# Recurrent heads of a two-block model on one core: full 32-bit gate products replaced by three products of high and low parts

## The reference

```python
def block_diag(x, w, b):          # 10 heads of 128 channels, w is (10, 128, 128)
    y = jnp.einsum('bshi,hij->bshj', x.reshape(bsz, s, h, i), w)
    return y.reshape(bsz, s, h * j) + b

def rglru_direction(xc, wa, ba, wx, bx, lam, reverse):
    r = jax.nn.sigmoid(block_diag(xc, wa, ba))
    i = jax.nn.sigmoid(block_diag(xc, wx, bx))
    log_a = -LRU_C * r * jax.nn.softplus(-lam)
    a = jnp.exp(log_a)
    b_in = jnp.sqrt(-jnp.expm1(2.0 * log_a)) * (i * x32)
    _, h = lax.associative_scan(_lin_combine, (a, b_in), axis=1, reverse=reverse)
```

## Time and profile before

| what | value |
|---|---|
| median of 3 runs | 3472.39 us |
| the profiled execution | 3469.35 us |
| its span, first to last instruction | 3468.0 us |
| TensorE (PE) busy | 3346.8 us, 97% of the span |
| VectorE (DVE) busy | 2045.6 us, 59% |
| ScalarE (ACT) busy | 1390.2 us, 40% |
| GpSimd (POOL) busy | 1317.9 us, 38% |
| mean granted TensorE clock | 0.993 of full speed |

### The profile page before, as it was taken

One profiled execution on the slowest core, in us unless ns is written; L12 is line 12 of the kernel. 1 busy time (PEld: TensorE's weight loads), 2 busy tenths in 40 slices (PEclk: granted clock), 3 DMA queues, 4 the chain that ended last, 5 costly groups with the idle time before them and its releaser, 6 DMA issues.

```text
span 3468.0 us, 48887 instructions
## 1 busy us (share of the span) xinstructions
PE 3346.8 (97%) x19926; PEld 2718.9 (78%) x19926; DVE 2045.6 (59%) x2689; ACT 1390.2 (40%) x2361; POOL 1317.9 (38%) x698
## 2 busy tenths in 40 slices
PE   7999999999989999999999999999999999999999
PEld 6788888897668778878887677777788877777787
DVE  3656737427754743345555538986544588888654
ACT  4443334344433544431113447772233343444212
POOL 3212222110024444454442116663344365656542
PEclk9999999999999999999999999999999999999999
DMA  5101111020036344442222322223465423333522
GB/s 153 43 19 47 42 33 48 26 62 7 1 110 213 107 138 143 142 174 97 97 97 87 103 90 67 82 83 107 163 196 172 135 88 109 106 111 106 188 96 81
DMA packets 343791, 344.40 MB, mean 99 GB/s; under 512 B 14661, under 2 KB 263937, under 8 KB 343568
## 3 DMA queue, kind: packets, MB, share of 16 engines
q1 hardware_dynamic: 328960, 307.00, 27.7%
q10 hardware_dynamic: 11520, 25.17, 1.9%
q0 software_dynamic: 3088, 9.10, 0.7%
HBM read 268.86 MB, written 72.35 MB: 98 GB/s over the span
## 4 chain that ended last, share of the span: by engine, by line


## 5 line engine op out<-in xcount | busy, mean ns | idle before, releaser
L461 POOL TENSOR_TENSOR weight_lo<-stage,weight_hi 128x1024 fp32r<-128x1024 f32 (+4 forms) x269 | 626.5, 2336 | 991.9 <-ACT weight_hi L439 963.1
L2459 DVE TENSOR_TENSOR x<-x,psum 128x512 f32<-128x512 f32 x416 | 283.9, 687 | 281.7 <-PE psum L403 271.2
L439 ACT ACTIVATE weight_hi<-stage 128x1024 fp32r<-128x1024 f32 (+4 forms) x329 | 299.7, 925 | 334.2 <-PE psum L403 289.8
L401 PE MATMUL psum<-hT_hi,weight_hi 128*128 128x512 f32 x1024 | 411.0, 401 | 1.5 <-DVE hT_lo L654 1.5
L402 PE MATMUL psum<-hT_lo,weight_hi 128*128 128x512 f32 x1024 | 400.2, 391 | 0.0
L403 PE MATMUL psum<-hT_hi,weight_lo 128*128 128x512 f32 x1024 | 400.1, 391 | 0.0
L401 PE MATMUL psum<-weight_hi,act_hi 128*128 128x512 f32 x864 | 337.3, 390 | 5.3 <-POOL act_lo L2407 4.2
L402 PE MATMUL psum<-weight_lo,act_hi 128*128 128x512 f32 x864 | 336.8, 390 | 0.0
L403 PE MATMUL psum<-weight_hi,act_lo 128*128 128x512 f32 x864 | 336.7, 390 | 0.0
L461 POOL TENSOR_TENSOR weight_lo<-sum,weight_hi 128x512 fp32r<-128x512 f32 (+1 forms) x114 | 238.2, 2099 | 233.8 <-ACT weight_hi L439 233.8
L401 PE MATMUL psum<-T_hi,weight_hi 128*128 128x512 f32 x608 | 238.6, 392 | 18.5 <-POOL weight_lo L461 14.5
(11 more groups left out here) (421 smaller groups left out, 7098.0 us busy)
## 6 DMA issues: line engine op xcount, KB each, us to landing
stage<-in_w_up SPq DMA_DIRECT2D x66, 512.0 KB, 4.3
stage<-in_w_in SPq DMA_DIRECT2D x64, 512.0 KB, 4.0
act_raw<-scratch_act SPq DMA_DIRECT2D x54, 512.0 KB, 5.2
stage<-in_w_ffn_up SPq DMA_DIRECT2D x48, 512.0 KB, 4.6
scratch_gates<-gate ACTq DMA_DIRECT2D x64, 256.0 KB, 2.0
gs<-scratch_gates SPq DMA_DIRECT2D x64, 256.0 KB, 3.1
stage<-in_w_out SPq DMA_DIRECT2D x32, 512.0 KB, 4.5
scratch_act<-out SPq DMA_DIRECT2D x64, 256.0 KB, 4.7
```

What stands on the lines that cost most here:

```text
L401: q.matmul(out, stat[0], mov[0], start=first, stop=False, skip_group_check=onto)
L439: a.q.activation(hi[:, part], src, ACT.Copy).then_inc(*S.w_hi.up(w))
L461: g.q.tensor_tensor(lo[:, part], src, hi[:, part].bitcast(F32), ALU.subtract).then_inc(*S.w_lo_pool.up(w))
L2459: v.q.tensor_tensor(dst, dst, K.bank(key), ALU.add).then_inc(*S.x.up(("f", f, g, t, n)))
```

## The change

The gate products go through `three`, so each of the 8 products of a head is three matmuls instead of one plain float32 call. For this a new step `head_split` stands at the head of each round of the loop, ahead of the next head's front. In it ScalarE makes the high parts of `xc` (128x1024) and of the four block weights (128x512), and GpSimd the two low parts by subtraction. The low parts of the block weights are written over the block weights themselves, which stay two buffers; the high parts and the low part of `xc` have one buffer each. The wait of the gate products for the load and for the convolution becomes a wait for ScalarE's and GpSimd's block weight parts.

```diff
 def pe_head_gate(K, j, i, h):
     b = K.open(key)
-    pe.wait_ge(S.wbd_load[j % 2], j)
-    pe.wait_ge(S.dve_op, ("xc", j))
-    pe.q.matmul(b, K.wbd[j % 2][:, i, :], K.xc[j % 2][:, h * HALF:(h + 1) * HALF], start=True, stop=True).then_inc(*S.mm.up(key))
+    pe.wait_ge(S.act_op, ("wbd_hi", j))
+    pe.wait_ge(S.pool_op, ("wbd_lo", j))
+    at = slice(h * HALF, (h + 1) * HALF)
+    three(pe.q, b, (K.wbd_hi[:, i, :], K.wbd_lo[j % 2][:, i, :]), (K.xc_hi[:, at], K.xc_lo[:, at]), True, True).then_inc(*S.mm.up(key))
+
+def act_head_split(K, j):
+    a, S = K.a, K.S
+    a.wait_ge(S.dve_op, ("xc", j))
+    if j:
+        a.wait_ge(S.mm, ("lru", j - 1, 3, 1))
+    a.q.activation(K.xc_hi[:, :], K.xc[j % 2][:, :], ACT.Copy).then_inc(*S.act_op.up(("xc_hi", j)))
+    a.wait_ge(S.wbd_load[j % 2], j)
+    a.q.activation(K.wbd_hi[:, :, :], K.wbd[j % 2][:, :, :], ACT.Copy).then_inc(*S.act_op.up(("wbd_hi", j)))
+
+def pool_head_split(K, j):
+    g, S = K.g, K.S
+    g.wait_ge(S.act_op, ("xc_hi", j))
+    g.q.tensor_tensor(K.xc_lo[:, :], K.xc[j % 2][:, :], K.xc_hi[:, :].bitcast(F32), ALU.subtract).then_inc(*S.pool_op.up(("xc_lo", j)))
+    g.wait_ge(S.act_op, ("wbd_hi", j))
+    g.q.tensor_tensor(K.wbd_lo[j % 2][:, :, :], K.wbd[j % 2][:, :, :], K.wbd_hi[:, :, :].bitcast(F32), ALU.subtract).then_inc(
+        *S.pool_op.up(("wbd_lo", j)))
...
     front(0)
     for j in range(NL):
+        o.do("head_split", j)
         if j + 1 < NL:
             front(j + 1)
```

More of the change, by code:

```diff
@@ L2987, in lay_out @@
     xn = [put("xn", [P, D], right=True) for _ in range(2)]
-    below_xn = m.hi
+    below_xn = xn_at = m.hi
     hT2 = pair("hT", [P, ND, S], right=True)
@@ L3059, in lay_out @@
     K.raw, K.raw2 = put("raw", [P, 16 + S + 16]), put("raw2", [P, 16 + S + 16])
+    wbd_at = m.lo
     K.wbd, K.wpool = [put("wbd", [P, 4, P]) for _ in range(2)], put("wpool", [P, 2, GDIM])
     K.sums = [put("sums", [P, 16 + S + 16]) for _ in range(2)]
+    K.wbd_hi = put("wbd_hi", [P, 4, P], F32R)
+    assert m.lo <= lows_at
+    m.lo = xn_at
+    K.xc_hi, K.xc_lo = put("xc_hi", [P, S], F32R), put("xc_lo", [P, S], F32R)
+    m.lo = wbd_at
+    K.wbd_lo = [put("wbd_lo", [P, 4, P], F32R) for _ in range(2)]
     K.counts, K.pooled, K.yb2 = K.gt[0], K.dc, K.th
@@ L4080, in scalar_program @@
             "store_rows": act_store_rows, "ple_mix": act_ple_mix, "x2_stored": act_x2_stored, "rates": act_rates,
-            "lru_edges": act_lru_edges, "u": act_u, "head_conv": act_head_conv, "head_gate": act_head_gate,
+            "lru_edges": act_lru_edges, "u": act_u, "head_conv": act_head_conv, "head_gate": act_head_gate, "head_split": act_head_split,
             "head_decay": act_head_decay, "head_scan": act_head_scan, "ya_stored": act_ya_stored,
@@ L4110, in gpsimd_program @@
 def gpsimd_program(K, steps):
-    part = {"param_load": pool_param_load, "param": pool_param, "weight": pool_weight, "gain": pool_gain,
+    part = {"head_split": pool_head_split, "param_load": pool_param_load, "param": pool_param, "weight": pool_weight, "gain": pool_gain,
             "handover": pool_handover, "gates_close": pool_gates_close, "rwkv_ready": pool_rwkv_ready,
```

## The result

The changed kernel takes 3592.9 us in the median of 4 runs (3591.22 to 3595.72), beside 3470.55 us for the kernel before: a ratio of 1.0351, 95% interval 1.0339 to 1.0363. Two executions in the later experiments (one of 5083.82 us, and one of the kernel before of 6647.53 us) were slow ones with a lower granted clock and are left out of the ratios. The profiled execution took 3595.72 us, with a span of 3594.4.

What follows compares the result with a forecast made beforehand. TensorE, busy 97% of the span, was taken as the bound. Head 0's delay, eight loops of 41.4 us and the last head made TensorE leave the branch 120.7 us later: 3469.35 + 120.7 = 3590, given as 3592 us; range 3558 to 3625.

Steps and rivals of the forecast that it cites:

- From the sum to the gate products: GpSimd's sum and store, weight tile's low part, low parts of xc and block weights: 3.27, 2.88, 2.88, 1.57, together 10.6 us.
- GpSimd is held in the wait: Three GpSimd subtractions before the gate products each held for a whole VectorE tap: 9.9 for 7.3 us, 3615 us; chance 0.12.
- The 0.5 that I took from the earlier trace: Extra time of a GpSimd subtraction beside a working VectorE: 2.88 us in place of 2.36 undisturbed.
- From the gate products to the square: 24 matmul parts with slow restart 7.7 us, then evacuation, table load, exp and tanh: GpSimd's square starts at 12.1 us.
- The two rivals on the clock: At TensorE's restarts: clock stays full, 3569 us, chance 0.13; clock low through all 24 parts or longer, 3617 us, chance 0.2.
- From the square to the sum: Elementwise chain from GpSimd's square to its sum: 18.7 us, read from heads 0 and 9, where GpSimd had been idle.
- Loop: One head, from one head_sum to the next: 10.6 + 12.1 + 18.7 = 41.4 us in place of 28.66.
- The first sum: Head 0's sum on GpSimd: forecast to start at 2108.2, which is 4.2 us later than before.
- The fifth rival: Steps not hidden but chain shorter, GpSimd undisturbed by 9 x 1.8 us, together with the full clock: 3553 us; chance 0.05.
- the split is hidden: At TensorE's wait for the low block weights: no price, the 14 us saving stays, 3458 us; chance 0.03.
- TensorE's own floor for a head falls to 27.2 us: TensorE's work per head: 24 parts cost 5.45 us for 6.87 before, 1.4 us less per head, 14 us over ten.
- The slow restart: After idling, TensorE runs at half pace for 4.8 us, so the 24 parts take 7.7 us in place of 5.45.

Runs made afterwards that it cites:

- the first experiment: Changed kernel with the split step of head j+1 moved behind the four head_mid operations of head j, ahead of root, scans and sum: 3502.7 us, ratio 1.0092.

## Why the prediction was right, and where its working was not

The time (3592 forecast, 3592.9 measured), the sign and the mechanism were right. The first of its steps needs one row more, VectorE's three taps beside GpSimd's subtractions in the changed kernel:

```profile
2238.69 7.87 DVE L2668 SCALAR_TENSOR_TENSOR xc<-raw,param,xc 128x1024 f32<-128x1024 f32 x3 [2.19 <-ACT xc L2661]
```

By its own steps:

- **From the sum to the gate products: 10.6 us forecast, 11.25 measured** (2236.58 to 2247.83). The terms missed in both directions. The weight tile's low part took 2.37 and not 2.88, the low part of xc 3.31 for 2.88, that of the block weights 2.24 for 1.57. In the last head, where no taps run, the last two took 2.34 and 1.26. One by one VectorE's taps start at 2238.69, 2240.04 and 2243.32 and take 1.31, 3.24 and 3.25 us. The weight tile (2239.83) met only the last 0.2 us of the first tap. The second tap ended 1.1 us behind the weight tile; the low part of xc, which had started beside that tap, took 1.0 us more than alone, and so did that of the block weights beside the third. So two subtractions were held by 1.0 us each, near to the 1.3 of the rival "GpSimd is held in the wait", and one not at all. The 0.5 that I took from the earlier trace rows was the mean of the same two cases: the two weight tiles of that row, one by one, took 2.42 and 3.39 us. The Trainium skill (SBUF — State Buffer, SBUF: two separate sides) calls the shared port pair an exclusive lock, and the trace agrees with it better than with my mean: who comes second waits for what is left of the other's instruction.
- **From the gate products to the square: 12.1 us forecast, 12.04 measured** in the head shown. The low clock lasted 4.0 us behind the restart there, where I had 4.8. That length varies: the 24 parts took 7.0 to 8.4 us from head to head, and the loops come out between 41.4 and 42.8 us. The two rivals on the clock are out: it neither stayed full nor stayed low for all parts.
- **From the square to the sum: 18.7 forecast, 18.67 measured.** Reading that chain off heads 0 and 9, where GpSimd had been idle before it, was what made the sum hold.
- **Loop: 41.4 forecast, 42.0 measured** over the first eight. The last was 40.17, with GpSimd not held.
- **The sum against its own time.** I worked out 3590 for an execution like the profiled one, and added 3.0 us for the median. The profiled execution of the changed kernel took 3595.7, 6 us more. TensorE left the branch at 2463.35 us and not at 2457.7, and that is the whole of it; that everything behind keeps its distance was right. The first sum was 2.3 us later than forecast, of which 1.7 lie ahead of the branch (the first taps began at 2069.10, before at 2067.41), eight loops added 4.7, and the last wait gave 1.3 back. The median of the four runs, 3592.9, lies 2.8 us below the profiled execution, where I had put it 3.0 above. That it comes within 1 us of the forecast is luck; the terms are good to about 6 us.
- **A slip in a rival.** The fifth rival takes 1.8 us a head for undisturbed GpSimd steps. Its own figures (2.36, 2.36 and 1.29 against 2.88, 2.88 and 1.57) make 1.3, so its time should read 3557 and not 3553. It bears on neither the forecast nor the range.
- **What failed: the price of the rival "the split is hidden", that is "none, so the 14 us stay: 3458".** The step behind it was the reading of what bounds the kernel, "TensorE's own floor for a head falls to 27.2 us", as if nothing else stood at 28.7. VectorE's 25.91 us in the earlier trace rows looked like slack. But with 0.74 us of wait for ScalarE's tap and 1.85 for GpSimd's square it closed a loop of 28.7 us with these engines: GpSimd goes from its sum (2190.02) through the store and two weight tiles to the square (2199.02, shown under the first experiment) with no wait but 0.30 us ahead of the store, 9.0 us, and from there it is 19.66 us to the next sum. With the split gone for nine heads (3474.3 us) nothing was gained, and with that loop relieved as well the time was 3460.65 us. Also the place ahead of the sum, where "GpSimd does idle 8.79 us", is not free: 3502.7 us.
- **The slow restart** was shown to cost time: keeping TensorE busy gave 16.7 us, where I had 23 for ten heads.

## What to carry to other kernels

A step added to an in-order queue is priced by what stands ahead of it there and by who waits behind it, not by its own 2 to 3 us: here two subtractions of GpSimd (3.31 and 2.24 us) behind the sum of the head before tied two loops that had run beside each other, and cost 12 us a head. An engine that is busy 100% of a stretch proves only that no other loop is longer, not that none is as long; before counting a saving on it, work out the longest chain through the other engines, waits included. And an idle gap of GpSimd isn't free where VectorE works in it: here the split cost 3.2 us a head there. A mean over instructions of one line can hide two cases, one held and one not: look at them one by one before using it as a price.

## What the runs showed of the hardware that I had not expected

- VectorE and GpSimd hold each other up in both directions. VectorE: the clamp (one tensor in) took 0.69 us alone and 1.7 to 2.8 where GpSimd held it; the product 1.2 and 2.3; the tap (two tensors and a scalar in) 1.285 and, in the median, 3.3. GpSimd: a subtraction of 128x1024 took 2.35 alone and 2.9 to 3.4 where VectorE held it; one of 128x512 1.27 alone and 1.7 to 2.3. The scans took 2.29 us throughout, but in none of these kernels did a GpSimd operation run beside one, so nothing is shown of them.
- 448 matmuls of no use made the kernel 16.7 us faster, because the useful ones behind them didn't have to run at the low clock.
